# A conditioning silu computed once ahead of the layer loop, and a square root at the end of the expert stage

## What is computed

```python
def modulation(cond, w, b):
    return jnp.split(jax.nn.silu(cond) @ w + b, N_MOD, axis=-1)

def rms_norm(x):
    xf = x.astype(jnp.float32)
    return (xf * lax.rsqrt(jnp.mean(xf * xf, axis=-1, keepdims=True) + RMS_EPS)).astype(x.dtype)

def modulate(x, shift, scale):
    return rms_norm(x) * (1 + scale) + shift

def trunk_layer(x, mod, lp, is_latent, ctx_k, ctx_v, s0):
    shift1, scale1, gate1, shift2, scale2, gate2 = mod
    h = modulate(x, shift1, scale1)
    z = h @ lp['w_in']
    ...                                  # RWKV, convolution, attention, merged by gates
    x = x + gate1 * (merged @ lp['w_o'])
    x = x + gate2 * peer_ffn(modulate(x, shift2, scale2), lp)
    return x, k, v, s_fin
```

## Time and profile before

| what | value |
|---|---|
| median of 3 runs | 5490.84 us |
| lowest and highest | 5488.35 and 5496.67 us |
| the profiled execution, its own time | 5486.03 us |
| its span, first to last instruction | 5484.3 us |
| TensorE's mean granted clock | 0.959 of full speed |
| busy: TensorE, VectorE, ScalarE, GpSimd | 87%, 71%, 26%, 28% |
| first pass, from | 12.2 us |
| second pass, from | 2746.5 us |

### The profile page before, as it was taken

One profiled execution on the slowest core, in us unless ns is written; L12 is line 12 of the kernel. 1 busy time (PEld: TensorE's weight loads), 2 busy tenths in 40 slices (PEclk: granted clock), 3 DMA queues, 4 the chain that ended last, 5 costly groups with the idle time before them and its releaser, 6 DMA issues. The chain is left out here.

```text
span 5484.3 us, 71055 instructions
## 1 busy us (share of the span) xinstructions
PE 4752.3 (87%) x26292; PEld 2587.3 (47%) x26292; DVE 3902.5 (71%) x9067; ACT 1431.5 (26%) x3630; POOL 1534.2 (28%) x1402
## 2 busy tenths in 40 slices
PE   8999888988888888888799998889888889898887
PEld 4556677533343434333355556775333334343332
DVE  4647777577787877777655477865777777777775
ACT  1123321322222222222211232213222222222222
POOL 0100000034444444444300000000344444444443
PEclk9999999999999999999999999999999999999999
DMA  4223511879999999999932244118899999999999
GB/s 160 73 76 148 209 60 34 331 297 427 412 426 427 415 427 412 427 416 421 422 120 71 74 184 175 58 64 305 336 427 413 421 424 412 427 415 427 412 424 412
DMA packets 309271, 1648.59 MB, mean 301 GB/s; under 512 B 34723, under 2 KB 48291, under 8 KB 143283
## 3 DMA queue, kind: packets, MB, share of 16 engines
q0 software_dynamic: 192768, 1367.95, 59.8%
q1 hardware_dynamic: 116148, 276.02, 13.7%
HBM read 1580.03 MB, written 63.82 MB: 300 GB/s over the span
## 5 line engine op out<-in xcount | busy, mean ns | idle before, releaser
L2324 PE MATMUL psum<-peer_rows,peer_diagonal 128*128 128x512 f32 x5120 | 2500.2, 623 | 514.3 <-ACT peer_diagonal L2386 513.2
L2257 POOL DMA_INDIRECT peer_rows<-in_peer_rows,look_up_index x1280 | 1471.8, 1150 | 2704.7 <-PE psum L2324 1637.8
L2467 DVE CUSTOM_DVE_ANT_0 peer_rows<-peer_rows,h_rows 128x1024 f32<-128x1024 f32 x1280 | 1552.3, 1225 | 480.7 <-DMA peer_rows<-in_peer_rows,look_up_index 467.9
L2324 PEld LDWEIGHTS psum<-peer_rows,peer_diagonal 128*128 128x128 f32 x5120 | 931.7, 197 | 1548.0 <-issue 833.5
L2380 ACT ACTIVATE peer_active<-peer_dots 128x2 f32<-128x2 f32 (+1 forms) x642 | 130.7, 204 | 2019.3 <-DVE peer_dots L2467 2019.2
L2386 ACT ACTIVATE peer_diagonal<-ident_sb,peer_weight 128x128 f32<-128x128 f32 x1280 | 444.2, 394 | 145.0 <-DVE peer_weight L2420 143.4
L2271 PEld LDWEIGHTS psum<-h_sb,query_weights 128*128 128x128 f32 x1184 | 232.8, 197 | 298.4 <-issue 298.4
L522 PE MATMUL psum<-shared,h_sb 128*128 128x512 f32 (+1 forms) x800 | 309.9, 549 | 0.0
L2420 DVE TENSOR_TENSOR peer_weight<-peer_active,peer_share 128x2 f32<-128x2 f32 (+1 forms) x642 | 103.8, 162 | 200.5 <-ACT peer_active L2380 200.5
L2271 PE MATMUL psum<-h_sb,query_weights 128*128 128x128 f32 x1184 | 233.2, 280 | 0.0
L522 PEld LDWEIGHTS psum<-shared,h_sb 128*128 128x128 f32 x800 | 152.0, 190 | 157.2 <-issue 153.1
(11 more groups left out here) (374 smaller groups left out, 5535.8 us busy)
## 6 DMA issues: line engine op xcount, KB each, us to landing
shared<-in_w_mod SPq DMA_DIRECT2D x22, 2048.0 KB, 14.7
shared<-in_w_in SPq DMA_DIRECT2D x12, 2048.0 KB, 8.2
shared<-scratch_rkv_scratch SPq DMA_DIRECT2D x30, 768.0 KB, 6.6
peer_rows<-in_peer_rows,look_up_index POOLq DMA_INDIRECT x1280, 12.1
scratch_rw_scratch<-rw_in_direction SPq DMA_DIRECT2D x20, 768.0 KB, 5.4
wkv_own<-scratch_rw_scratch SPq DMA_DIRECT2D x20, 768.0 KB, 6.2
next_gate_weights<-in_w_gate POOLq DMA_DIRECT2D x20, 512.0 KB, 4.6
scratch_rw_scratch<-shared SPq DMA_DIRECT2D x10, 1024.0 KB, 6.0
```

Source lines behind the costliest of these rows:

```text
L2257: nc.gpsimd.indirect_dma_start(rows[spot][:, :], None, t.dram["peer_rows"], bass.IndirectOffsetOnAxis(ap=index[j % 4][:, k:k + 1], axis=0) ...
L2324: last = nc.tensor.matmul(t.bank[2 * (i % 2) + c], diagonal[k % DIAGONALS][:, :], rows[spot][:, D + c * 512:D + (c + 1) * 512], start=(j = ...
L2467: v.tensor_tensor_reduce(rows[spot][:, 0:D], rows[spot][:, 0:D], h[:, :], 1.0, 0.0, ALU.mult, ALU.add, dots[b][:, k:k + 1]).then_inc(s["do ...
```

## The change

The sigmoid of the condition and its product move out of the begin stage into the block `start`, so they are done once and no longer in each pass; the waits for them on TensorE and VectorE go from the begin stage. `start` has two more semaphores of its own for it and a third, `cond_loaded`, for the condition's load, so that its ScalarE can begin ahead of the tokens' load; SyncE there waits for the other three. The tile `begin_sigmoid` goes (the sigmoid is written into `t.silu` and multiplied in place). At the end of ScalarE's list in the expert stage stands a square root of the constant one into a new tile `next_root`, which nothing reads. No transfer is added, removed or moved.

```diff
--- before.py
+++ after.py
@@ -242,7 +242,6 @@
         biases = t.y_attn[:, :, :].rearrange("p j n -> p (j n)")[0:1, 0:4 * 512]
         bias = [biases[:, c * 512:(c + 1) * 512] for c in chunks]
         mod_rows = [sbuf(f"mod_rows{b}", MOD_HALF) for b in range(2)]
-        sig = sbuf("sigmoid", KD, 2)
         unwritten = t.y_rw[:, :, :].rearrange("p j n -> p (j n)")
         square = t.y_conv[:, :, :].rearrange("p j n -> p (j n)")[:, 0:D]
         normed = [unwritten[:, b * D:(b + 1) * D] for b in range(2)]
@@ -279,7 +278,6 @@
                                                    normed[i % 2][:, (half * 4 + k) * P:(half * 4 + k + 1) * P], t.ident[:, :])
                     last.then_inc(s["turned"], 1)
 
-            pe.wait_ge(s["silu"], 1)
             pe.wait_ge(s["bias_loaded"], 16)
             for q, tiles in enumerate(TURNED_BEHIND):
                 if q < CHUNKS_AHEAD:
@@ -295,7 +293,6 @@
 
         @block.scalar
         def _(act):
-            nc.scalar.activation(sig[:, :, :], t.cond[:, :, :], ACT.Sigmoid).then_inc(s["sigmoid"], 1)
             for i in range(BY_SCALAR):
                 if i:
                     act.wait_ge(s["squared"], i)
@@ -325,8 +322,6 @@
         @block.vector
         def _(dve):
             v = nc.vector
-            dve.wait_ge(s["sigmoid"], 1)
-            v.tensor_tensor(t.silu[:, :, :], t.cond[:, :, :], sig[:, :, :], ALU.mult).then_inc(s["silu"], 1)
             for i in range(BY_SCALAR, TILES):
                 v.tensor_tensor_reduce(normed[i % 2], t.x[:, i, :], t.x[:, i, :], 1.0, 0.0, ALU.mult, ALU.add, total[:, i:i + 1]).then_inc(s["summed"], 1)
             dve.wait_ge(s["summed"], TILES - BY_SCALAR)
@@ -363,7 +358,7 @@
             dve.wait_ge(s["vector_modulated"], 12)
 
 
-BEGIN = ("sigmoid", "silu", *MOD_SIGNALS, "bias_loaded", "weights_loaded0", "weights_loaded1", "summed", "squared", "mean", "root", "inverse", "normed", "turned", "scalar_wrote", "vector_wrote", "scalar_modulated",
+BEGIN = (*MOD_SIGNALS, "bias_loaded", "weights_loaded0", "weights_loaded1", "summed", "squared", "mean", "root", "inverse", "normed", "turned", "scalar_wrote", "vector_wrote", "scalar_modulated",
          "vector_modulated")
 
 
@@ -2389,6 +2384,7 @@
                     if i:
                         act.wait_ge(s["added"], i)
                     nc.scalar.copy(out[:, :].rearrange("p (c n) -> p c n", c=2), t.psum[:, 2 * (i % 2):2 * (i % 2) + 2, :]).then_inc(s["emptied"], 1)
+            nc.scalar.activation(t.next_root[:, :], t.ones[:, 0:1], ACT.Sqrt)
 
         @block.vector
         def _(dve):
@@ -2496,7 +2492,7 @@
 
 SCRATCH = {"rkv_scratch": (TILES * CORE_ROWS, 3 * W), "rw_scratch": (NTOK, RW_BLOCKS, W), "out_scratch": (2, NTOK, W),
            "gate_scratch": (GATE_BLOCKS, P, NTOK)}
-OUTER_STAGES = (("start", ("loaded", "zeroed", "chunk_ahead0", "chunk_ahead1")), ("finish", ("stored",)))
+OUTER_STAGES = (("start", ("cond_loaded", "sigmoid", "silu", "loaded", "zeroed", "chunk_ahead0", "chunk_ahead1")), ("finish", ("stored",)))
 STAGES = (("begin", BEGIN), ("project", PROJECT), ("qk", QK),
           ("attention", ATTENTION), ("rwkv_inputs", RWKV_INPUTS), ("wkv", WKV), ("rwkv_output", RWKV_OUTPUT),
           ("context", CONTEXT), ("peer", PEER))
@@ -2569,6 +2565,7 @@
         t.x = sbuf("x_sb", [P, TILES, D])
         t.h = sbuf("h_sb", [P, KD, NTOK])
         t.table_start = sbuf("table_start", [P, 1])
+        t.next_root = sbuf("next_root", [P, 1])
         t.shared = stack.enter_context(nc.sbuf_tensor("shared", [P, KD * D], F32, side="right"))
         t.chunk_places = [t.shared[:, q * KD * 512:(q + 1) * KD * 512].rearrange("p (k n) -> p k n", k=KD) for q in range(2)]
         t.in_weights = t.chunk_places
@@ -2579,17 +2576,26 @@
         with nc.Block() as block:
             @block.sync
             def _(sp):
-                sp.dma_start(t.cond[:, :, :], d["cond"]).then_inc(s["loaded"], 16)
+                sp.dma_start(t.cond[:, :, :], d["cond"]).then_inc(s["cond_loaded"], 16)
                 sp.dma_start(t.ident[:, :], d["square_constants"][0, :, :]).then_inc(s["loaded"], 16)
                 sp.dma_start(t.ones[:, :], d["square_constants"][1, :, :]).then_inc(s["loaded"], 16)
                 sp.dma_start(t.x[:, :, :], d["x"].rearrange("(t p) n -> p t n", p=P)).then_inc(s["loaded"], 16)
                 load_chunks_ahead(sp, t, 0)
-                sp.wait_ge(s["loaded"], 64)
+                sp.wait_ge(s["loaded"], 48)
 
             @block.vector
             def _(dve):
                 nc.vector.memset(t.table_start[:, :], 0.0).then_inc(s["zeroed"], 1)
+                dve.wait_ge(s["sigmoid"], 1)
+                nc.vector.tensor_tensor(t.silu[:, :, :], t.cond[:, :, :], t.silu[:, :, :], ALU.mult).then_inc(s["silu"], 1)
                 dve.wait_ge(s["zeroed"], 1)
+                dve.wait_ge(s["silu"], 1)
+
+            @block.scalar
+            def _(act):
+                act.wait_ge(s["cond_loaded"], 16)
+                nc.scalar.activation(t.silu[:, :, :], t.cond[:, :, :], ACT.Sigmoid).then_inc(s["sigmoid"], 1)
+                act.wait_ge(s["sigmoid"], 1)
         with nc.Fori(0, DEPTH) as layer:
             layer_stages(nc, t, stages, layer)
         s = stages["finish"]
```

## The result

The changed kernel takes 5539.44 us (median of six runs, 5537.89 to 5545.53), the kernel before 5490.35 (median of six). The ratio is 1.0093, 95% interval 1.0082 to 1.0104: 49 us slower. The forecast was 5490.7 us within 5481 to 5502, no change that can be measured. It was wrong, and by far more than the 3.0 us that the prediction gave the added instructions at most.

What follows compares the result with a forecast made beforehand. The prediction took expert-row transfers to bound the kernel, the two expert stages being 58% of the span. Its terms, -0.1 + 0 + 0 + 0 + 0 us on the median 5490.84, gave 5490.7 us, range 5481 to 5502.

Steps and rivals of the forecast that it cites:

- The places in memory: Expert rows' eight places move to 32 bytes past a multiple of 256: cost taken as 0, ends 12.4 us either way.
- a fixed part of 9.7 ns: Time per row beyond its bytes, read as equal for 8 KB expert rows and 2 KB begin-stage rows, so place costs nothing.
- The prediction's own sign of being wrong: Expert stages differing from 1590 and 1588 us by over 5 us each would mean that places in memory count.
- 12.4 us: Bound on the expert stages' places: one step of 32 bytes in 8192, 1/256 of 1590 + 1588 us.
- Rival (b): Expert stages' gathers pay for their new place, 1/256 more for each row: 5503.1 us; chance 8%.
- the 0.1 taken: Second pass's head: without the silu wait, TensorE's first matmul waits for the bias and gains 0.1 us.
- rival (a): Second pass's head: the bias lands early and the pass gains its bound of 1.4 us: 5489.4 us; chance 10%.
- The loads stay in the begin stage: A ScalarE table load remains in both passes, since the loop's two entries carry different tables; cost 0.
- Rival (d): Second pass's norm starts without any load, up to 2.7 us earlier, TensorE no sooner: 5490.7 us; chance 18%.
- The root at the end of the expert stage: Added load and root, 1.49 us per pass, covered by 2.5 us until VectorE's last addition: 0; without cover 3.0 together.
- the silu ahead of the loop: Start block: silu done at 4.4 us at the latest, tokens land at 11.8; cover 7.4 us, so cost 0.
- the norm's room: Second pass's begin stage: first normalised tile is done 1.4 us before TensorE's transposes, so a shorter norm gains nothing.

Runs made afterwards that it cites:

- The instructions at the old places: The whole change, but the added square root is written into a tile the stage already has, so no tile is added: 5489.38 us, 1.0001 to the kernel before.
- the last experiment: One more square root in the start block, against the kernel of the change with later bias wait and nearly all tiles on multiples of 256: 5475.37 us, 0.9980.
- The later wait for the bias: Whole change without a new tile, plus TensorE's bias wait moved from ahead of the first product to the bias's own matmuls: 5482.39 us, 0.9993 to the kernel before.
- the two traces: The change without a new tile with TensorE's bias wait moved later, 5482.39 us; the same with nearly all tiles on multiples of 256, 5477.54 us.

## Why the prediction was wrong

**The places in memory: the step that failed.** The prediction saw that the new tile moves the expert rows off a multiple of 256, named the mechanism and the 3178 us that it would act on, and then priced it at 0, with 12.4 us as the end. The 0 came from two rates: 8 KB rows on the boundary and 2 KB rows off it, from which it read a fixed part of 9.7 ns "in both" and concluded that the place costs nothing. That reading was empty. Two measurements fix a price per byte and one fixed part, and whatever the short rows paid for their place went into that fixed part; with two lines there is nothing left over to compare. The runs supply the third measurement: 2 KB rows on the boundary take 80.7 ns. With it the line through the two lengths on the boundary is (310.6 - 80.7) / 6144 = 0.0374 ns a byte and 4.1 ns fixed. The other 4.2 of the short rows' 84.9 ns are the price of their place. The two lengths differ in kind as well, gathers by GpSimd and plain loads by SyncE, so the 4.1 is an estimate; the 4.2 is not touched by that. The prediction's own sign of being wrong, expert stages that differ by over 5 us each, is what came.

**The bound was mis-sized.** 12.4 us, one step of 32 bytes in 8192, was taken from the size of the move. The price does not grow with that size; it is about 5 ns a row at each of the distances tried, from 32 to 224. 1280 gathers of 128 rows on 16 engines are 10240 rows an engine; 49.1 us over these is 4.8 ns. Rival (b), with 8%, was the case that came, at four times the loss that it was given, and the range left it out.

**The rest held.** The instructions at the old places are worth 1.0001 (0.9992 to 1.0010), the forecast's nothing. The first matmul of the second pass waits for the bias and starts 1.70 us before the change, 1.75 after it and 1.71 at the old places behind the bias's issue: a gain of 0, against the 0.1 taken, and rival (a), the early bias, falls. The loads stay in the begin stage in both passes, as both entries of the loop are not alike; the last experiment made them alike and both loads went, at a stage's start and under a table brought in by the stage ahead. Rival (d) falls for the kernel as changed. The rule of the Trainium skill (ScalarE activation tables: per-element evaluation and per-set limits, Table sets in the compiler and the runtime) that loads are placed per block, read as each block starting over, would have kept the loads there. The trace of that last kernel, with no load in the begin stage of either pass, speaks against that reading. The root at the end of the expert stage is covered, ending 2.5 us ahead of VectorE; so is the silu ahead of the loop.

**A cover that was thin.** The prediction put the norm's room at 1.4 us and ScalarE's queue off the path. That holds as long as the bias holds TensorE. The later wait for the bias showed the room used up: the copy behind the root is the next in line, 1.0 and 1.3 us late in the two traces.

## What to carry to other kernels

Count a new tile as a change to every tile that is allocated behind it: where a stage is bound by transfers, look at the places that they fill, before and after, and keep them on multiples of 256 bytes. Here that is worth 4 to 5 ns a row, 0.9% of the kernel for 8 KB rows. A price that is read from two rows which differ in more than one respect (here the length, the place and the kind of transfer) is no bound; a third row, or a run that changes the one respect alone, has to separate them.

## What the runs showed that was not expected

- A gather of 8 KB rows into places 32, 64, 128 or 224 bytes past a multiple of 256 costs 0.8 to 1.0% of this kernel, with intervals that overlap, and 414 to 416 GB/s in place of 421 to 422. Rows of 2 KB by plain transfers went from 386 to 406 GB/s when their places were put on such a multiple, and at 394 where one tile of three was.
- With the two ways into the loop carrying different tables, the begin stage had two loads, the first ahead of squares that never had one of their own before; with the same table on both, none. One square root of 0.2 us and one load of 1.28 us ahead of the loop removed four loads in it, two in each pass.
